# A two-block transformer kernel on one core: in the gate tiles, GpSimd makes the low halves of the weight slabs, and VectorE and ScalarE share the low one-hot rows six to two instead of four to four

## The reference

```python
def peer_ffn(x, w_q, sub_keys, u, v):
    q = (xi @ w_q).reshape(n, PEER_HEADS, 2, PEER_KEY_DIM)
    s = jnp.einsum('nhpc,hpkc->nhpk', q, sub_keys).astype(jnp.float32)
    ts, ti = lax.top_k(s, PEER_TOPK)
    ...
    idx = jnp.take_along_axis(cand_i, best_p, axis=-1)
    gate = jax.nn.softmax(best_s, axis=-1)
    act = jax.nn.gelu(jnp.einsum('nd,nhkd->nhk', xi, u[idx]).astype(jnp.float32), approximate=False)
    return jnp.einsum('nhk,nhkd->nd', (gate * act).astype(xi.dtype), v[idx])
```

## Time and profile before

| what | value |
|---|---|
| median of three runs | 2384.38 us |
| span of the profiled execution | 2384.3 us |
| PE busy in the span | 2317.8 us (97%) |
| DVE busy | 1687.0 us (71%) |
| ACT busy | 1105.2 us (46%) |
| POOL busy | 559.1 us (23%) |
| gate tiles, from octet 2 on | 860.7 to 1031.1 us |
| DVE busy from 860.71 to 1033 us | 164.67 of 172.29 us |
| PE busy there | 164.86 us |

### The profile page before, as it was taken

The page is one execution under the profiler, slowest core; times in us unless marked ns, Lnnn a source line. Parts: engine busy times, 40 slices in busy tenths (PEclk is TensorE's granted clock), DMA queues, the critical chain, the costliest instruction groups (busy, mean ns, idle before and its releaser), DMA issues.

```text
span 2384.3 us, 38223 instructions
## 1 busy us (share of the span) xinstructions
PE 2317.8 (97%) x13522; PEld 1292.8 (54%) x13522; DVE 1687.0 (71%) x2995; ACT 1105.2 (46%) x1677; POOL 559.1 (23%) x418
## 2 busy tenths in 40 slices
PE   7999999999999999999999999999999999999998
PEld 4446764655555566665555555564444444444454
DVE  5327765587999979978888888877443448776234
ACT  4266443766666778853333333344422234333233
POOL 0001001577888632225222222113000010000001
PEclk9999999999999999999999999999999999999988
DMA  5200022588899669999999999923233323333321
GB/s 182 80 27 1 1 71 80 178 280 310 314 317 332 223 194 359 360 356 365 375 362 357 363 355 362 366 79 115 89 115 97 106 80 106 106 99 105 105 71 53
DMA packets 164872, 470.67 MB, mean 197 GB/s; under 512 B 17745, under 2 KB 70737, under 8 KB 163985
## 3 DMA queue, kind: packets, MB, share of 16 engines
q1 hardware_dynamic: 109312, 289.48, 35.6%
q0 software_dynamic: 36864, 134.23, 15.3%
q10 hardware_dynamic: 18576, 45.36, 4.8%
HBM read 421.56 MB, written 47.45 MB: 197 GB/s over the span
## 4 chain that ended last, share of the span: by engine, by line
PE 77%; DVE 15%; ACT 2%; issue 2%; DMA 2%; DVEq 1%; POOL 1%; SPq 0%; ACTq 0%
PE psum L554 23%; PE psum L555 23%; PE psum L556 23%; DVE arena L2125 4%; DMA arena<-in_urows,arena 1%; DVEq L2050 1%; PE psum L436 1%; DVE arena L528 1%; PE psum L1142 1%; PE psum L1019 1%; PE psum L1143 1%; PE psum L897 1%; DVE arena L1921 1%; DVE arena L2063 1%; DVE arena L2061 1%
## 5 line engine op out<-in xcount | busy, mean ns | idle before, releaser
L554 PE MATMUL psum<-arena 128*128 128x384 f16 (+2 forms) x3648 | 1259.6, 347 | 18.0 <-DVE arena L485 7.6
L555 PE MATMUL psum<-arena 128*128 128x384 f16 (+2 forms) x3648 | 1262.5, 346 | 0.0
L556 PE MATMUL psum<-arena 128*128 128x384 f16 (+2 forms) x3648 | 1255.8, 346 | 0.0
L554 PEld LDWEIGHTS psum<-arena 128*128 128x128 f16 x3648 | 354.2, 97 | 350.2 <-issue 34.6
L556 PEld LDWEIGHTS psum<-arena 128*128 128x128 f16 x3648 | 353.2, 97 | 322.6 <-issue 4.3
L555 PEld LDWEIGHTS psum<-arena 128*128 128x128 f16 x3648 | 353.4, 97 | 309.7 <-issue 4.8
L528 DVE SCALAR_TENSOR_TENSOR arena<-arena 128x1024 f16<-128x1024 f32 x216 | 265.8, 1234 | 276.7 <-ACT arena L515 275.7
L515 ACT ACTIVATE arena<-arena 128x1024 f16<-128x1024 f32 x216 | 226.4, 1052 | 237.3 <-PE psum L556 226.0
L1680 ACT ACTIVATE arena<-arena 128x1024 f16<-128x1024 f32 x128 | 135.5, 1059 | 299.4 <-PE psum L556 281.8
L534 POOL TENSOR_TENSOR arena<-arena 128x1024 f16<-128x1024 f32 x104 | 228.9, 2201 | 93.5 <-ACT arena L523 92.1
L447 POOL TENSOR_TENSOR arena<-arena 128x512 f32<-128x512 f32 x15 | 19.8, 1320 | 890.4 <-ACT arena L401 890.4
(11 more groups left out here) (259 smaller groups left out, 2221.0 us busy)
## 6 DMA issues: line engine op xcount, KB each, us to landing
arena<-in_w SPq DMA_DIRECT2D x320, 512.0 KB
arena<-in_v SPq DMA_DIRECT2D x128, 512.0 KB
early_activations<-arena ACTq DMA_DIRECT2D x124, 192.0 KB
arena<-early_activations SPq DMA_DIRECT2D x124, 192.0 KB
gate_matrix<-arena ACTq DMA_DIRECT2D x5, 4096.0 KB
arena<-gate_matrix SPq DMA_DIRECT2D x32, 640.0 KB
arena<-in_xT SPq DMA_DIRECT2D x4, 512.0 KB, 6.3
arena<-in_urows,arena POOLq DMA_INDIRECT x128
```

The source lines that it names most:

```text
L554: nc.tensor.matmul(ps, a_h, b_h, start=first, stop=False)
L555: nc.tensor.matmul(ps, a_h, b_l, start=False, stop=False)
L556: return nc.tensor.matmul(ps, a_l, b_h, start=False, stop=last)
```

## The change

Three things change, all in the gate tiles.

1. The 29 slabs whose low half VectorE made between the octets go to GpSimd. It first multiplies the slab by 64 in place (`tensor_scalar`, f32 to f32, 128 x 1024), waits for that by a semaphore of its own (`low_scaled`), and then subtracts (`tensor_tensor`, 128 x 1024, f16 out). Behind each slab it issues one of the row fetches that stood alone in its queue before.
2. VectorE's instruction for `hot_low` makes six of eight rows (128 x 768) instead of four (128 x 512).
3. ScalarE makes two rows instead of four.

Behind the tiles VectorE waits once until GpSimd has made the last of its slabs, and goes on with low halves as before.

```diff
+OCT_ACT = 2
+LOW_TILES = N_U + TILES_AT + SLOTS - 1
+LOW_TAIL = LOW_TILES + TILE_SLABS
@@ ScalarE
-                for j in range(OCT // 2, OCT):
+                for j in range(OCT - OCT_ACT, OCT):
@@ VectorE, one_hots
-                half = OCT // QUAD // 2
-                nc.vector.tensor_tensor(hot_low[b][:, 0:half], hot_slab[b][:, 0:half], col(gatel)[:, 0:half],
+                most = OCT // QUAD - OCT_ACT // QUAD
+                nc.vector.tensor_tensor(hot_low[b][:, 0:most], hot_slab[b][:, 0:most], col(gatel)[:, 0:most],
                                         ALU.mult).then_inc(hot_out, 1)
@@ VectorE, tile_turn
-                    if t == 0 and i == 1:
-                        dve.wait_ge(low_cut, cuts.n)
-                    if i:
-                        cuts.upto(N_U + e + (i - 1 + (i - 1) // 4 + ((i - 1) % 4 == 3)) // 2 + 3)
-                    elif t:
-                        cuts.upto(N_U + e - 1 + 3)
@@ VectorE, behind the tiles
+            dve.wait_ge(low_cut, LOW_TAIL)
             for e in range(TAIL_AT, NK):
@@ GpSimd
-            for k in range(HEAD_PICKS + ROWS_G, 2 * PICKS):
+            for n in range(LOW_TILES, LOW_TAIL):
+                x = n - LOW_TILES
+                pool.wait_ge(high_cut, n + 1)
+                nc.gpsimd.tensor_scalar(wraw[:, slot(n), :], wraw[:, slot(n), :], WS, None, ALU.mult).then_inc(low_scaled, 1)
+                pool.wait_ge(low_scaled, x + 1)
+                nc.gpsimd.tensor_tensor(wl[:, slot(n), :], wraw[:, slot(n), :], wh[:, slot(n), :],
+                                        ALU.subtract).then_inc(low_cut, 1)
+                own_fetch(HEAD_PICKS + ROWS_G + x)
+            for k in range(HEAD_PICKS + ROWS_G + TILE_SLABS, 2 * PICKS):
                 own_fetch(k)
```

More of the change, by code:

```diff
@@ L90 @@
 LOW_POOL = N_PQ + SLOTS - 1
+TILE_SLABS = GT * TILE_U - 1
+LOW_TILES = N_U + TILES_AT + SLOTS - 1
+LOW_TAIL = LOW_TILES + TILE_SLABS
 TURN_BANKS = (2, 3, 0)
@@ L639, in build @@
         low_out = sem("low_out")
+        low_scaled = sem("low_scaled")
         hot_slab_out, hot_out, g_done, g_out = sem("hot_slab_out"), sem("hot_out"), sem("g_done"), sem("g_out")
@@ L2146, in _ @@
                        if 0 < h < PH - 1 else None)
-            cuts.n += 2 * PH + TILES_AT
+            cuts.n = LOW_TAIL
             dve.wait_ge(idxT_out, 3)
@@ L2166, in one_hots @@
                 nc.vector.tensor_tensor(hot_high[b], hot_slab[b], col(gateh), ALU.mult)
-                half = OCT // QUAD // 2
-                nc.vector.tensor_tensor(hot_low[b][:, 0:half], hot_slab[b][:, 0:half], col(gatel)[:, 0:half],
+                most = OCT // QUAD - OCT_ACT // QUAD
+                nc.vector.tensor_tensor(hot_low[b][:, 0:most], hot_slab[b][:, 0:most], col(gatel)[:, 0:most],
                                         ALU.mult).then_inc(hot_out, 1)
             def tile_turn(t):
-                e = TILES_AT + t * TILE_U
                 picks = HEAD_PICKS + t * TILE_PICKS
```

## The result

The changed kernel takes 2428.14 us (median of five runs, 2426.14 to 2432.40), the kernel before beside it 2384.38 us: 1.0179 times as long, 95% interval 1.0165 to 1.0193. The forecast was 2422.6 us, range 2396 to 2450.

A forecast was written before the change was run, and what follows sets the result against it. VectorE was taken to bound the gate tiles; 138.1 us of work plus 71.1 us of GpSimd holds made 209.2 instead of 170.4 us, less 0.5 for an earlier start: 2384.3 + 38.3 = 2422.6 us, range 2396 to 2450.

The forecast's parts named there:

- The bound before: Gate tiles from octet 2: VectorE's own work 164.0 of 170.4 us, TensorE 157, so VectorE bound by 13 us.
- The work that leaves and comes: VectorE in the tiles: low halves (31.9 us) and waits (6.4) go, wider `hot_low` adds 6.0, leaving 138.1 us.
- The subtraction's hold: Tiles: each GpSimd subtraction holds VectorE's one-hots 1.90 us, before hiding, for 29 slabs.
- hidden: Tiles: dot products cover part of GpSimd's holds, 0.27 us for a hold, about 0.5 for a slab.
- The scaling's hold: Tiles: each GpSimd scaling, taken as 1.25 us long, holds VectorE 1.05 us before hiding; possible 0 to 1.90.
- GpSimd isn't the bound: Tiles: GpSimd needs 136 us and some waiting, within VectorE's 209, so it does not set the pace.
- TensorE's clock: Rival in the tiles: idle TensorE drops to the lower clock, 105 us more, 2527 us; chance 0.02. Short falls hidden.
- What was costed at nothing: Tiles: low halves about 5.5 us after high halves instead of 2.4, next loads, wait behind the tiles: no cost.
- The sum: Tiles 209.2 us instead of 170.4, 38.8 more; octet 2 about 0.5 earlier; 2384.3 + 38.3 = 2422.6 us.
- TensorE as the bound: Rival in the tiles: holds stay below 19 us together, TensorE's 157 us sets the pace, 2371 us; chance 0.06.
- Scaling without a hold: Rival in the tiles: scaling holds nothing, 30 us less, 2392 us; chance 0.09, shared with most of both holds hidden.
- Late fetches: Rival in the tiles: row fetches behind GpSimd's work delay each dot 1.4 us, 40 us more, 2463 us; chance 0.06.

The follow-up runs named there:

- the split alone: Kernel before, with low one-hot rows shared six to two between VectorE and ScalarE, VectorE still making all low halves of the tiles: tiles 170.4 us, ratio 0.9994.
- the memset: Changed kernel with GpSimd's scaling replaced by a memset of the same size, which reads nothing: tiles 187.8 us, ratio to the kernel before 1.0069.
- the aligned subtractions and all low rows on VectorE: Changed kernel, but ScalarE scales, GpSimd's subtractions wait for VectorE's dot products (two further on), VectorE makes all eight low rows: tiles 173.1 us, ratio 1.0010.
- the run with ScalarE scaling: Changed kernel with ScalarE scaling the tiles' slabs in place and GpSimd only subtracting: tiles 191.1 us, ratio to the kernel before 1.0085.
- the run with the fetch in the middle: Changed kernel with the row fetch between scaling and subtraction instead of behind the subtraction: tiles 216.7 us, one run, 2430.6 us.

## Why the prediction was right

**The bound before.** VectorE at 164.0 of 170.4 us, TensorE 13 us below. Right as far as the change asks. The run with the split alone shows the limit of that reading: 6 us more on VectorE cost nothing, because its waits for ScalarE's high halves gave way (9.0 to 3.7 us). VectorE and ScalarE were the bound together.

**The work that leaves and comes.** 138.1 us were forecast for octets and dots. Measured: 212.0 - 73.1 - 0.4 = 138.5. The wider `hot_low` was put at 0.13 us each; undisturbed it takes 0.55 us where 512 columns took 0.42. The 5.5 us that undoing it gave are a mixture of work, holds and idle time, and don't confirm the 6.0.

**The subtraction's hold.** 1.90 us less 0.25 hidden, 1.65 for each, 47.9 in all; measured 48.6.

**The scaling's hold.** 1.05 less 0.25, 23.2 in all; measured 24.5. The number is right by luck. I took 1.25 us for the duration and the hold from it. The scaling lasts 2.79 us undisturbed, 2.97 in the mean, more than twice as long, and is above the subtraction that I had named as the upper end. It holds VectorE for its first 0.9 us only, so the prediction's rule that the two exclude each other for as long as either lasts doesn't fit it. 24 scalings met a one-hot. Twelve lengthened it by 0.31 to 0.84 us and twelve, right behind a fetch, by 1.31 or 1.32; the mean of 1.02 beside my 1.05 is made of these two kinds, and I had given the fetch no part in it. Had the scaling held as long as it runs, less 0.2 us, the forecast would have been some 40 us too low. The estimate from the Trainium skill, "GPSIMD Engine Reference", section 3.1, 0.9 to 1.0 us, is refuted as a duration by the 2.79.

**GpSimd isn't the bound.** Right, but 136 us were forecast for it and it took 188 of 212; with a scaling of that length little was left.

**TensorE's clock.** The granted clock was 0.94 over the tiles instead of 0.99, 0.91 in most stretches of 20 us. That is no short fall, as the prediction had it, but a lower mean through most of the tiles. It cost nothing there: VectorE was the bound, and the idle time of TensorE (37.0 us of waits) took it up.

**What was costed at nothing.** In the waits of the tiles TensorE names neither GpSimd nor a slab's low half, and ScalarE waits for no load. The later low halves cost nothing, as forecast.

**The sum.** The tiles were forecast at 209.2 us and took 212.0, so 38.8 more became 41.6. Octet 2 began 2.0 us earlier where 0.5 was forecast. The span grew by 40.1. The medians lie 43.8 apart; the interval of the ratio is 39 to 46 us. The changed kernel's profiled run took 2426.14 us for a span of 2424.4; 1.7 us lie outside the span. I had taken the span before for the whole time. The forecast against the span (2422.6) was 1.8 us below it.

**The rivals.** TensorE as the bound: no. Scaling without a hold: no, though the memset shows what it would have been worth, 24.2 us. Late fetches: not in the changed kernel, where VectorE has 0.4 us of idle time; they came with the aligned subtractions and all low rows on VectorE (7.4 us), where each fetch stood behind the wait for the subtraction before.

## What to carry to other kernels

Before work is moved from VectorE to an idle GpSimd, look at what VectorE will run beside it. If its instructions have both operands in SBUF, they pay for what GpSimd reads, here 1.68 us for a subtraction that took 1.14 us off; an idle engine isn't a free one. Look in the trace for a place where the two already meet: one-hots of 2.52 and 2.37 us, where 0.69 and 0.42 are usual, told this result beforehand.

Where the work has to be there, let it start when VectorE turns to an instruction with an operand in PSUM. That took the holds from 53 to 20 us. The time came down only to about that of the kernel before (1.0023), until the waits that then showed up were dealt with too (0.9987).

## What the runs showed of the hardware that I had not expected

- GpSimd's `tensor_scalar` on 128 x 1024 f32, in place, lasts 2.79 us, longer than its `tensor_tensor` on two such tensors (2.15 us). On 512 columns it lasts 1.5 us.
- It holds a one-hot of VectorE, which has two SBUF operands, for its first 0.9 us, 0.4 to 0.5 us for 512 columns. The rest of it disturbs nothing. The subtraction holds for the first 2.0 of its 2.15 us.
- A one-hot under way mostly gets through, and GpSimd's instruction is the one that grows (in the run with ScalarE scaling the subtraction grows from 2.15 to as much as 2.66 us, and no one-hot under way is longer). It isn't safe where GpSimd's instruction follows a row fetch within 0.03 us. Then 12 of 17 in the changed kernel and 14 of 14 in the run with the fetch in the middle were held, and the time they had already run, 0.39 us in most, was lost on top of the hold (1.31 and 2.41 us together).
